# The last expert's rows added by one-hot products, a bias table made early, and the borders around it re-ordered, in a two-block transformer forward pass

## What is computed

```
weights, experts = top-2 of the router, per row      # 512 rows in layer 0, 256 in layer 1
x[row] += sum over its two experts of  w * gate * (silu(h[row] @ w1[e]) * (h[row] @ w3[e])) @ w2[e]
```

## Time and profile before

| what | us |
|---|---|
| median of three runs | 2123.66 (2121.88 to 2123.98) |
| the profiled execution, its own time | 2122.17 |
| its span | 2120.3 |
| TensorE busy | 1955.7 (92% of the span) |
| VectorE (DVE) busy | 647.4 (31%) |
| ScalarE (ACT) busy | 370.5 (17%) |
| GpSimd (POOL) busy | 322.0 (15%) |
| TensorE in the chain that ended last | 65% |
| transfers in that chain | 22%, of it moe weights 20% |

### The profile page before, as it was taken

The page is one execution under the profiler, slowest core; times in us unless marked ns, Lnnn a source line. Parts: engine busy times, 40 slices in busy tenths (PEclk is TensorE's granted clock), DMA queues, the critical chain, the costliest instruction groups (busy, mean ns, idle before and its releaser), DMA issues.

```text
span 2120.3 us, 34138 instructions
## 1 busy us (share of the span) xinstructions
PE 1955.7 (92%) x14829; PEld 1223.9 (58%) x14829; DVE 647.4 (31%) x1508; ACT 370.5 (17%) x821; POOL 322.0 (15%) x264
## 2 busy tenths in 40 slices
PE   5999999999999969999999988988879989989998
PEld 4566575555555445546555444444457677665884
DVE  1234382222222232115331111111136031037752
ACT  3133320000000011114310000000021130042131
POOL 0125412000000000115210000000120060040120
PEclk8999999999999999999999999999989999999999
DMA  9563299999999989317399999999964423427221
GB/s 361 151 208 122 88 383 393 427 427 426 427 424 426 427 327 283 111 40 279 140 383 426 426 423 427 426 422 426 393 240 143 146 80 125 153 78 201 81 92 60
DMA packets 131760, 584.22 MB, mean 276 GB/s; under 512 B 19082, under 2 KB 32490, under 8 KB 106896
## 3 DMA queue, kind: packets, MB, share of 16 engines
q1 hardware_dynamic: 113216, 550.26, 66.0%
q10 hardware_dynamic: 12272, 25.26, 3.3%
q0 software_dynamic: 6112, 6.39, 0.9%
HBM read 572.29 MB, written 23.22 MB: 281 GB/s over the span
## 4 chain that ended last, share of the span: by engine, by line
PE 65%; DMA 22%; DVE 5%; issue 3%; POOL 2%; ACT 2%; SPq 1%; POOLq 0%; DVEq 0%; ACTq 0%
DMA RG<-in_moe_w 20%; PE banks L1545 12%; PE banks L2527 8%; PE banks L1570 5%; PE banks L2099 4%; PE banks L2529 4%; PE banks L1093 4%; PE banks L1521 3%; PE banks L684 3%; PE banks L2101 3%; PE banks L2728 3%; PE banks L2939 2%; POOL AR L921 2%; PE banks L814 2%; PE banks L842 1%
## 5 line engine op out<-in xcount | busy, mean ns | idle before, releaser
L1545 PE MATMUL banks<-RG,HT 128*64 128x256 f32 x3616 | 426.6, 389 | 34.6 <-DMA RG<-in_moe_w 32.7
L1545 PEld LDWEIGHTS banks<-RG,HT 128*64 128x64 f32 x3616 | 250.1, 134 | 218.1 <-DMA RG<-in_moe_w 55.0
L1775 POOL DMA_INDIRECT y_rows<-AR x64 | 63.6, 994 | 871.0 <-DVE AR L1584 870.1
L1554 DVE TENSOR_TENSOR AR<-AR,banks 128x256 f32<-128x256 f32 x64 | 38.6, 603 | 484.3 <-ACT AR L1550 433.1
L1570 PE MATMUL banks<-RG,AR 128*64 128x512 f32 x752 | 171.7, 598 | 3.1 <-DVE AR L1563 3.1
L2527 PE MATMUL banks<-HT,RG 128*128 128x256 f32 x768 | 168.0, 380 | 0.8 <-ACT HT L553 0.8
L2527 PEld LDWEIGHTS banks<-HT,RG 128*128 128x128 f32 x768 | 145.4, 190 | 22.8 <-issue 2.4
L1550 ACT ACTIVATE AR<-banks 128x256 f32<-128x256 f32 x64 | 24.5, 383 | 749.9 <-PE banks L1545 749.9
L1521 PE MATMUL banks<-AR 128*128 128x256 bf16 (+1 forms) x1152 | 149.2, 277 | 1.7 <-DVE AR L1509 1.5
L1521 PEld LDWEIGHTS banks<-AR 128*128 128x128 bf16 x1152 | 108.2, 98 | 33.4 <-issue 18.3
L1570 PEld LDWEIGHTS banks<-RG,AR 128*64 128x64 f32 x752 | 49.8, 136 | 93.8 <-issue 83.6
(11 more groups left out here) (480 smaller groups left out, 2397.5 us busy)
## 6 DMA issues: line engine op xcount, KB each, us to landing
RG<-in_moe_w SPq DMA_DIRECT2D x160, 2048.0 KB, 23.9
AR<-in_moe_w SPq DMA_DIRECT2D x32, 2048.0 KB, 23.1
RG<-in_ada_w SPq DMA_DIRECT2D x24, 2048.0 KB, 9.3
RG<-in_attn_w_in SPq DMA_DIRECT2D x20, 2048.0 KB, 7.9
RG<-in_odd_w_in SPq DMA_DIRECT2D x6, 2048.0 KB, 20.3
RG<-in_ssm_w_in SPq DMA_DIRECT2D x4, 2048.0 KB, 9.3
AR<-y_rows ACTq DMA_DIRECT2D x6, 1024.0 KB, 7.6
RG<-in_even_w_in SPq DMA_DIRECT2D x2, 2048.0 KB, 23.1
```

The lines of the kernel that those rows point to most:

```text
L1545: m = pe.matmul(p[64 * h:64 * h + 64, 256 * i:256 * i + 256], x[:, k, :], w[:, h, k], start=k == 0, stop=k == 7, skip_group_check=True)
L1775: g.indirect_dma_start(y, off, E.Y[b], None, bounds_check=2047, oob_is_err=False).then_inc(*event)
```

## The change

The last expert's rows (e = 31) no longer pass through DRAM. DVE keeps them in a tile YL. From the row numbers of expert 31's slots it makes a one-hot matrix LP behind expert 27 (`dve_last_hot`), and TensorE multiplies LP with YL, one tile of 128 rows at a time (`pe_last`: two products with 64 contraction rows each, 512 columns). DVE adds the result from PSUM to XS with a weight WL that is zero for rows not routed to expert 31 (`dve_last`); WL comes from three more steps in `dve_weights` and one in the routing. So that `y_rows` holds zeros for expert 31, a scatter of a cleared Y tile is issued at expert 28.

ACT issues the loads of the first two tiles ahead of the silu of expert 31, when the scatters of 29 and 30 and the zeros have landed, in four transfers of 0.5 MB (`act_combine_first`). In layer 0 the other two tiles' loads follow behind down 31. DVE's order behind layer 0 is: the last expert's rows of tiles 0 and 1, the overflow test, joins 0 and 1, L474, both scales and diagonals, evictions, and only then tiles 2 and 3. TensorE makes 36 keep-warm products instead of 26 and 4, turns tiles 0 and 1, starts the odd queries, and puts the last additions and the turns of tiles 2 and 3 between the four parts of the queries. SP issues the first odd weight when tiles 0 and 1 have landed, and the second when all have.

The distance bias is made in layer 0's projection stage. One product of 384 columns follows the first projection weight, its copy on 16 partitions is stored by ACT as 16 x 128 x 256 elements, 2 MB, already skewed and reversed by the reading pattern, and two loads behind down 31 of layer 1 bring it to the place where the masks read it. The identity with reversed rows, the staging tile and the 16 reversals with their copies are gone.

The diff, cut to its core ("..." marks what is left out):

```diff
-        FRD = nc.dram_tensor("dist_bias", [16, 384], F).ap()
+        FRD = nc.dram_tensor("dist_bias", [16, 128, 256], F).ap()
...
+        OHT, RB2 = ar(13 * KK, 384), ar(13 * KK + 384, 16)
...
+                if ci == 0:
+                    pe.wait_ge(*at("even_loads", 8))
+                    pe.matmul(PS[7][0:16, 0:384], RB2[0:32], OHT[0:32], start=True, stop=True).then_inc(*ev("dist_row"))
...
+                if x == 1:
+                    pe.wait_ge(*at("dist_row_out"))
...
+                if ci == 0:
+                    act.wait_ge(*at("dist_row_out"))
+                    src = bass.AP(FR[:].tensor, FR[:].offset + 127, [[384, 16], [-1, 128], [1, 256]])
+                    act.dma_start(FRD, src).then_inc(*dm("dist_store"))
...
+            v.wait_ge(*at("dist_row"))
+            v.tensor_copy(FR[0:16], PS[7][0:16, 0:384]).then_inc(*ev("dist_row_out"))
...
+                self.YL = u(4.5, 512) if l == 0 else self.Y[1]
+                self.LP = u(6, 128 * nt) if l == 0 else u(4.5, 128 * nt)
...
-                self.Z = [ar((9 + 2 * t) * KK, 2, D) for t in range(4)] if l == 0 else [ar(10 * KK, 2, D), ar(15 * KK, 2, D)]
+                places = ((0, 1), (2, 12), (13, 14), (15, 16)) if l == 0 else ((10, 3), (15, 16))
+                self.Z = [[ar(i * KK, D) for i in pair] for pair in places]
...
+                v.tensor_scalar(E.LM, E.ek, 31.0, None, EQ)
...
+        def dve_last_hot(v, E):
+            l, n, tokens = E.l, 2 * E.nt, E.TG[:, 31:32]
+            wrap, token = E.LQ[:, 0:1], E.LQ[:, 1:2]
+            v.wait_ge(*at("selected", l, 6, 7))
+            v.wait_ge(*at("tabled", l, 6))
+            vstep(v, v.tensor_scalar(wrap, tokens, 512.0 - BIG, -512.0, ALU.is_ge, MUL))
+            vstep(v, v.scalar_tensor_tensor(out=token, in0=wrap, scalar=BIG, in1=tokens, op0=ADD, op1=ADD))
+            vstep(v, v.tensor_scalar(E.TB, IOT[:, 0:n], -64.0, token, MUL, ADD))
+            v.tensor_tensor(E.LP.rearrange("p (a b) -> p a b", b=64), bc(IOT[:], 1, n), bc(E.TB, 2, 64),
+                            EQ).then_inc(*ev("last_hot", l))
+
+        def last_banks(E, t):
+            return ((0, 1), (4, 6), (2, 3), (4, 5))[t]
+
+        def pe_last(pe, E, t):
+            if t == 0:
+                pe.wait_ge(*at("last_hot", E.l))
+                pe.wait_ge(*at("y_out", E.l, 31))
+            for h in range(2):
+                r = slice(64 * h, 64 * h + 64)
+                m = pe.matmul(PS[last_banks(E, t)[h]], E.LP[r, 128 * t:128 * t + 128], E.YL[r, :], start=True, stop=True)
+            m.then_inc(*ev("last_out", E.l, t))
+
+        def dve_last(v, E, t, event):
+            v.wait_ge(*at("last_out", E.l, t))
+            for h in range(2):
+                x = XS[:, t, 512 * h:512 * h + 512]
+                ins = v.scalar_tensor_tensor(out=x, in0=PS[last_banks(E, t)[h]], scalar=E.WL[:, t:t + 1], in1=x, op0=MUL,
+                                             op1=ADD)
+            ins.then_inc(*event)
...
+                if e == 31:
+                    act_combine_first(act, E)
...
-            v.tensor_tensor(E.WT[:, :, 1], E.WT[:, :, 0], E.gw, MUL)
+            vstep(v, v.tensor_tensor(E.WT[:, :, 1], E.WT[:, :, 0], E.gw, MUL))
+            vstep(v, v.tensor_tensor(E.LM, E.LM, E.WT, MUL))
+            vstep(v, v.tensor_reduce(E.WL, E.LM, AX, ADD))
...
-                dve_y_out(v, E, b, ev("y_out", l, e))
+                if e == 28:
+                    v.wait_ge(*at("clear_store", l))
+                dve_y_out(v, E, E.Y[b] if e < 31 else E.YL, b, ev("y_out", l, e))
...
+                if e == 27:
+                    clear = E.at[28] % 2
+                    v.wait_ge(*at(f"y_store{clear}", l, 26))
+                    v.memset(E.Y[clear], 0.0).then_inc(*ev("rows_clear", l))
+                    dve_last_hot(v, E)
...
+                if e == 28:
+                    g.wait_ge(*at("rows_clear", l))
+                    pool_scatter(g, E, 31, b, dm("clear_store", l))
+                if e == 31:
+                    break
...
-                e.wait_ge(*at(f"y_store{b}", E.l, 30 + b))
+                e.wait_ge(*at(f"y_store{b}", E.l, 30 - b))
...
-        def act_combine(act, E):
-            for t in range(E.nt):
-                act.dma_start(E.Z[t], Y2D.rearrange("(c r) d -> r c d", c=2)[128 * t:128 * t + 128]).then_inc(
-                    *dm(f"z_load{t}", E.l))
+        def act_z_load(act, E, t, kind, *key):
+            for c in range(2):
+                act.dma_start(E.Z[t][c], Y2D[512 * c + 128 * t:512 * c + 128 * t + 128]).then_inc(*dm(kind, *key, c))
+
+        def act_combine_first(act, E):
+            act.wait_ge(*at("clear_store", E.l))
+            for b in range(2):
+                act.wait_ge(*at(f"y_store{b}", E.l, 30 - b))
+            for t in range(2):
+                act_z_load(act, E, t, f"z_load{t}", E.l)
...
+            for t in range(2):
+                pe_last(pe, E0, t)
-            experts_done(pe, E0)
...
-            act_combine(act, E0)
+            act.wait_ge(*at("down", 0, 31))
+            for t in range(2, 4):
+                act_z_load(act, E0, t, f"z_load{t}", 0)
...
+            for t in range(2):
+                dve_last(v, E0, t, ev("last_added", 0, t))
...
         def pe_odd_begin(pe):
             pe_odd_cols(pe)
-            for t in range(4):
-                pe_keep(pe, (26, 4, 0, 0)[t], 3)
...
+            pe_keep(pe, 36, 3)
+            for t in range(2):
+                pe_odd_turn(pe, t)
+            pe.wait_ge(*at("ada_cols", 1, 3))
+            pe_last(pe, E0, 2)
+
+        def act_odd_squares(act, i):
+            act.wait_ge(*at("joined_rows", i))
...
+        def act_odd_turned(act, t):
+            act.wait_ge(*at("turned", "mix1", t, 0))
+            for k in range(odd_on_act(t)):
...
+            ins.then_inc(*ev("turned_out", "mix1", t, 0))
 
         def act_odd_begin(act):
-            act.dma_start(AB[:, 4:12], I["ada_b_pad"][1][:, 4:12]).then_inc(*dm("ab2_load"))
             act.activation(ST[:, 62:63], IDN[:, 0:1], ACT.Sqrt)
-            for i in range(4):
-                act.wait_ge(*at("joined_rows", i))
...
-                if i in (1, 2):
-                    act_root(act, ("mix1", i - 1), at_=i - 1)
+            for i in range(2):
+                act_odd_squares(act, i)
+                act_root(act, ("mix1", i), at_=i)
+            act.wait_ge(*at("ada_cols", 1, 3))
+            for t in range(2):
+                act_odd_turned(act, t)
+            for i in range(2, 4):
+                act_odd_squares(act, i)
             act_root(act, ("mix1", 3), n=2, at_=2)
-            act.wait_ge(*at("ada_cols", 1, 3))
-            for t in range(4):
...
         def dve_odd_begin(v):
-            for i in range(4):
-                v.wait_ge(*at(f"z_load{i}", 0))
-                dve_join(v, E0, i, ev("joined_rows", i))
-                if i == 0:
-                    dve_odd_raw(v, 1)
-                if i == 1:
-                    dve_odd_cols(v)
-                if i >= 2:
-                    dve_rstd(v, ("mix1", i - 2), D, at_=i - 2)
-                    dve_diagonal(v, i - 2)
+            for i in range(2):
+                v.wait_ge(*at("last_added", 0, i))
+                dve_odd_join(v, i, ev("joined_rows", i))
+            dve_odd_raw(v, 1)
+            for i in range(2):
+                dve_rstd(v, ("mix1", i), D, at_=i)
+                dve_diagonal(v, i)
+            dve_odd_cols(v)
+            v.wait_ge(*at("ada_cols", 1, 3))
+            for i in range(2):
+                dve_odd_turned(v, i)
+            for i in range(2, 4):
+                dve_odd_join(v, i, ev("z_joined", i))
+                v.wait_ge(*at("z_joined", i))
+                dve_last(v, E0, i, ev("joined_rows", i))
             v.wait_ge(*at("squares", ("mix1", 2)))
             dve_rstd(v, ("mix1", 3), D, n=2, at_=2)
             for t in (2, 3):
                 dve_diagonal(v, t)
-            v.wait_ge(*at("ada_cols", 1, 3))
-            for t in range(4):
-                v.wait_ge(*at("turned", "mix1", t, 1))
...
+            for t in (2, 3):
+                dve_odd_turned(v, t)
 
...
         def pe_odd(pe):
+            for t in range(2):
+                for b in range(2):
+                    pe.wait_ge(*at(*turned_out("mix1", t, b)))
             for c in range(3):
                 for j in range(4):
+                    if c == 0 and j == 2:
+                        pe.wait_ge(*at("joined_rows", 2))
                     pe_odd_part(pe, c, 0, j)
+                    if c == 0 and j == 0:
+                        pe_last(pe, E0, 3)
+                    if c == 0 and j == 2:
+                        for t in (2, 3):
+                            pe_odd_turn(pe, t)
+                if c == 0:
+                    for t in (2, 3):
+                        for b in range(2):
+                            pe.wait_ge(*at(*turned_out("mix1", t, b)))
...
         def act_odd(act):
-            act.wait_ge(*at("turned", "mix1", 3, 1))
```

(33 more changed lines are left out.)

156 lines of the change are left out of this document (70 added, 86 removed).

## The result

The changed kernel takes 2125.44 us (median of 12 runs, 2123.38 to 2128.28), the kernel before 2121.94 in 12 runs beside it (2118.09 to 2124.46). The ratio is 1.0018 with a 95% interval of 1.0010 to 1.0025: the medians differ by **+3.5 us**, where -3.7 was forecast.

What follows compares the result with a forecast made beforehand. DMA bytes were taken to bound the expert stages, TensorE or small steps the rest. Terms 0.64 + 0.5 + 0.6 + 2.0 - 6.0 - 1.4 = -3.7 us gave 2120.0; range 2114.0 to 2126.5, own case 2116.5 to 2122.5.

Steps and rivals of the forecast that it cites:

- Bias loads (-6.0): Second expert stage: taking out two 1024 KB dist_bias loads saves 6.0 us, all on the path.
- the table (+0.64): First layer's projection: one extra bias product in TensorE's gapless run costs 0.64 us.
- Masks, clears, one-hot: Small DVE steps cost +0.5, zero scatters of both stages +0.6; memset and one-hot behind expert 27 hidden.
- The border behind layer 0 (+2.0): After layer 0's experts: L474's successor at 781.9, the key product 2.0 us later.
- The test, priced at 1.1: Both borders: DVE's test for overflow blocks, formerly hidden under transfers, takes 1.1 us ahead of the joins.
- rival A: First border: rows delay the last modulation weight to 784, +4.5 on the sum, 2124.5 us; chance 0.22.
- the 72 keep-warm instructions: First border, TensorE: keep-warm products ahead of the turns take 10.5 us, with the diagonals long ready.
- The border behind layer 1 (-1.4): After layer 1's experts: silu 2.1 late, yet the first join starts 1.4 us earlier.
- B: Both borders: test 0.3 and four issues 1.5, bias loads giving 6.5; 2116.6 us; chance 0.22.
- C: Second expert stage: bias bytes were hidden anyway, only 1 of 6 us comes back, 2125.0; chance 0.08.
- D: Last expert's rows still pass through DRAM, only with overflow blocks, and the chain holds none; chance 0.02.
- The store of the table: First layer: 2 MB store from 16 partitions estimated at 20 us; modulation products waiting behind it would show the prediction wrong.

Runs made afterwards that it cites:

- e1: Kernel before with only the bias table moved: made in the first layer's projection, loaded behind down 31 of layer 1; 2116.70 us, ratio 0.9980.
- e12: Kernel before, without the code of layer 0's overflow blocks; 2121.46 us, ratio 1.0002.
- e3: Changed kernel without layer 0's overflow blocks and their tests on all five engines; 2123.36 us, ratio 1.0007.
- e2: Changed kernel with ACT's scatter wait and four loads behind the silu of expert 31 instead of ahead, in both layers; 2119.89 us, ratio 0.9992.
- e11: Changed kernel with silu 31 ahead of the loads and all layer 0 rows loaded only behind the last modulation product; 2126.76 us, ratio 1.0023.
- e4: Changed kernel with 12 keep-warm products instead of 36 ahead of the turns; 2119.09 us, ratio 0.9988.
- e5: Changed kernel with the first odd weight waiting for all four tiles' rows, as before the change; 2121.82 us, ratio 1.0002.
- e6: Changed kernel with the loads of tiles 2 and 3 issued only behind the last modulation product; 2123.72 us, ratio 1.0011.
- e7: Changed kernel without layer 0's overflow blocks and with tiles 2 and 3 loaded behind the last modulation product; 2117.26 us, ratio 0.9981.
- e10: Changed kernel: silu 31 first, 12 keep-warm products, tiles 2 and 3 loaded behind ACT's squares, first odd weight behind last modulation product; 2113.15 us, ratio 0.9960.

## Why the prediction was wrong

**Bias loads (-6.0) and the table (+0.64): right.** -5.79 in the changed kernel's stage, -6.2 in e1's, and 4.2 (2.3 to 5.9) in e1's time against 5.3. The table's product took 0.81.

**Masks, clears, one-hot: not refuted.** With the table they bring expert 31 of layer 0 1.68 later; the three terms that lie there made 1.44. That the two are so near is luck: e1, with the table alone, has it 2.74 later, and the same code scatters by 3.1 us.

**The border behind layer 0 (+2.0): the step that failed.** It measured +8.25. By its own steps:
- The silu was 2.0 late against 2.7; that step held. What I didn't follow was the idle TensorE behind it: down 31 stood in the sum at its old 3.65 and took 5.35, since the clock had fallen. Missed 1.7.
- The test, priced at 1.1 by SP's row. DVE took 4.64 behind its additions. SP skips blocks too, but its row was no guide to DVE. Missed 3.5, though off the path in the end, as TensorE is later still: with that, the 1.7 and the 1.68 by which all of it comes late, less 0.7 for the silu, the joins start at 782.77 instead of 776.7.
- TensorE's own test was not priced at all, and this is what sets L473. I had its product "done by 781.9" and asked only when the weight lands. It stood 5.08 and 3.28, and the product ended at 792.3. In the kernel before TensorE was idle 6.60 ahead of that product, and the row names the landing of y_rows as what ended it. That the change takes this wait away and keeps the jump that lay inside it was the question to ask (e12: without the jump the product still waited for the scatter). I costed the test as "formerly hidden" for DVE alone.
- The last modulation weight was rival A, at 0.22. I gave it a landing of 784, and e3 measured 785.0 and e2 786.9. Its time (2124.5 against 2125.44) agrees by luck: in the changed kernel the stops cover the weight, and A prices neither them nor the clock. By the rule of the Trainium skill (DMA: Bandwidth & Descriptors, Queues, rings and completion order) that the prediction drew on, the landing would be near 784; these landings agree in size, and so does 26.8 in e11, where no rows are beside it. I gave A no more than 0.22 because "the first set alone costs just the slack"; but both sets of rows come ahead of the landing.
- In my favour, the 72 keep-warm instructions took 8.20, not 10.5.

**The border behind layer 1 (-1.4): right in kind, short in size.** -0.79. The silu was 2.06 late as predicted and the test, priced at 1.1, cost nothing there, for DVE's join follows its additions at once; but down 31 ran at the lower clock, 5.87 for 3.65. Without the late silu the gain is 3.4 (e2). So the idea of the change, to save the latency of one scatter and one load, works where its cover is in place.

**The other rivals.** B (quicker borders) needed a test of 0.3 and fell with it. C fell with e1. D is out: the products and additions of L1626 and L1633 stand in every trace.

**Sum.** -3.7 was forecast and +1.6 came between the profiled spans, 5.3 us apart. The first border makes +6.3 of that (8.25 against 2.0), the second +0.6, the steps ahead +0.2; the odd layer gives 1.24 back and the rest 0.6. The 1.24 lies inside what the odd layer scatters in traces of the same code. How a stop divides between the test, the jump and the fetch is open, and so is what the data beside it adds.

**The store of the table.** It took 24.4 us to land, 86 GB/s for 2.1 MB, and no modulation product of the first layer waits for a weight behind it. The Trainium skill (SBUF — State Buffer, Door 1: The DMA port swizzle) gives 104 GB/s for 16 partitions, from which the prediction estimated 20 us; by that rule, the trace agrees in size.

## What to carry to other kernels

When a change removes a wait, list what else the engine did inside it: a test, a jump over code that isn't run, a table load. That work was free and now stands on the path. Price a skip over unused code by the first instructions behind it on the same engine, not by another engine's test: here it cost 8.4 us on TensorE, 4.64 on DVE and, in layer 1, nothing. And before a wait is put ahead of a small step of a chain (here ACT's silu), follow TensorE's idle time through it: 2 us of delay cost another 1.7 to 2.2 in clock. Issue early only what is awaited early: rows and a weight that nobody needed yet held up the two transfers that were needed.

## What the runs showed of the hardware that I had not expected

- An engine that jumps over unused code can stop twice behind it: TensorE 2.77 and 1.79 us with DMA quiet, 5.08 and 3.28 beside 367 GB/s, nothing without the code. The second stop comes in the middle of a product, behind the same 36th instruction in nine traces. DVE's jump in layer 1 cost nothing.
- The granted clock was 0.50 (1.2 GHz) from 782 to 788 us of the changed kernel, behind the 5.08 us stop. Behind an idle gap of 3.15 us ahead of the transpose down 31 took 1.7 us longer, and behind one of 2.57 in e4 as well; behind one of 1.12 it did not.
- 4 MB of rows beside it moved the landing of one 2 MB weight from 26.8 us behind its issue to between 36.0 and 38.9 (e2 to e5); 2 MB of them moved it to between 32.2 and 33.7 (e6, e7, e10).
